# Chunk stage of a retention / RWKV-7 / mixture-of-experts layer: the kept state enters PSUM by a product with the identity, and VectorE scales the sum in one operation

## The reference, cut to what matters

```python
def step(s, xt):
    wt, kt, vt, kkt, at = xt[:5]
    sa = jnp.einsum('bhvk,bhk->bhv', s, -kkt)
    s = (s * wt[:, :, None, :] + sa[..., None] * (kkt * at)[:, :, None, :]
         + vt[..., None] * kt[:, :, None, :])
    return s, jnp.einsum('bhvk,bhk->bhv', s, xt[5])
```

## Time and profile before

| | |
|---|---|
| median of three runs | 4093.11 us |
| lowest, highest | 4092.32, 4101.29 us |
| span of the profiled execution, first to last instruction | 4080.9 us |
| TensorE (matmul) busy | 3706.6 us, 91% |
| VectorE busy | 2310.9 us, 57% |
| ScalarE busy | 1890.7 us, 46% |
| GpSimd busy | 663.1 us, 16% |
| chunk stage | about 1192 to 2192 us of the span |

### The profile page before, as it was taken

The page is one execution under the profiler, slowest core; times in us unless marked ns, Lnnn a source line. Parts: engine busy times, 40 slices in busy tenths (PEclk is TensorE's granted clock), DMA queues, the critical chain, the costliest instruction groups (busy, mean ns, idle before and its releaser), DMA issues. The chain is left out here.

```text
span 4080.9 us, 96351 instructions
## 1 busy us (share of the span) xinstructions
PE 3706.6 (91%) x40786; PEld 3108.5 (76%) x40786; DVE 2310.9 (57%) x3792; ACT 1890.7 (46%) x3029; POOL 663.1 (16%) x637
## 2 busy tenths in 40 slices
PE   7999999999978888888887979997699999999993
PEld 6778878888867777777786867785588888888883
DVE  6533523434348888888786964555544444454545
ACT  5533434433336665666565443333244444444443
POOL 1000000000012222222220333200011111111111
PEclk9999999999989999999999989998799999999996
DMA  7555554444442222322323366644366666666668
GB/s 279 192 181 192 180 192 157 150 160 158 150 129 77 80 70 74 81 81 76 92 65 115 103 228 225 198 169 184 137 214 216 213 218 207 214 207 214 213 211 298
DMA packets 378754, 673.61 MB, mean 165 GB/s; under 512 B 90428, under 2 KB 261540, under 8 KB 360712
## 3 DMA queue, kind: packets, MB, share of 16 engines
q1 hardware_dynamic: 351368, 580.69, 42.9%
q0 software_dynamic: 27008, 87.46, 7.3%
HBM read 524.89 MB, written 143.15 MB: 164 GB/s over the span
## 5 line engine op out<-in xcount | busy, mean ns | idle before, releaser
L112 PE MATMUL fro__acc<-fro__hT_hi,fro__wh 128*128 128x512 f32 (+1 forms) x1608 | 625.2, 389 | 11.8 <-DVE fro__hT_lo L2692 8.9
L113 PE MATMUL fro__acc<-fro__hT_hi,fro__wl 128*128 128x512 f32 (+1 forms) x1608 | 613.2, 381 | 0.0
L114 PE MATMUL fro__acc<-fro__hT_lo,fro__wh 128*128 128x512 f32 (+1 forms) x1608 | 613.1, 381 | 0.0
L2698 DVE TENSOR_TENSOR fro__wl<-prj__w,fro__wh 128x1024 fp32r<-128x1024 f32 x201 | 246.2, 1225 | 637.5 <-ACT fro__wh L2481 637.5
L2109 DVE TENSOR_TENSOR fin__wl<-fin__raw,fin__wh 128x4096 fp32r<-128x4096 f32 x96 | 424.7, 4424 | 316.3 <-ACT fin__wh L2053 316.3
L2053 ACT ACTIVATE fin__wh<-fin__raw 128x4096 fp32r<-128x4096 f32 x96 | 348.4, 3629 | 190.4 <-PE exp__acc L114 190.3
L112 PE MATMUL exp__acc<-fin__wh,exp__xh 128*128 128x512 f32 x1024 | 400.1, 391 | 0.7 <-DVE exp__xl L2114 0.7
L114 PE MATMUL exp__acc<-fin__wl,exp__xh 128*128 128x512 f32 x1024 | 398.7, 389 | 0.0
L113 PE MATMUL exp__acc<-fin__wh,exp__xl 128*128 128x512 f32 x1024 | 398.7, 389 | 0.0
L112 PEld LDWEIGHTS fro__acc<-fro__hT_hi,fro__wh 128*128 128x128 f32 x1608 | 303.7, 189 | 77.8 <-issue 22.2
L113 PEld LDWEIGHTS fro__acc<-fro__hT_hi,fro__wl 128*128 128x128 f32 x1608 | 303.8, 189 | 59.0 <-issue 3.6
(11 more groups left out here) (461 smaller groups left out, 7648.3 us busy)
## 6 DMA issues: line engine op xcount, KB each, us to landing
fin__raw<-in_w_x SPq DMA_DIRECT2D x96, 2048.0 KB
prj__w<-in_w_z SPq DMA_DIRECT2D x201, 512.0 KB, 3.9
s_zT<-fro__pool SPq DMA_DIRECT2D x128, 256.0 KB, 4.3
fro__wm<-in_w_mod POOLq DMA_DIRECT2D x16, 1024.0 KB, 5.5
mix__gate<-s_zT SPq DMA_DIRECT2D x64, 256.0 KB, 3.9
prj__xin<-in_tokens SPq DMA_DIRECT2D x18, 512.0 KB, 5.6
rwc__kS<-s_kS SPq DMA_DIRECT2D x36, 256.0 KB, 3.1
rwc__kkn<-s_kkn SPq DMA_DIRECT2D x36, 256.0 KB, 3.2
```

The costliest lines, as they stand in the source:

```text
L112: pe.matmul(out, sh, mh, start=first, stop=False)
L113: pe.matmul(out, sl, mh, start=False, stop=False)
L114: return pe.matmul(out, sh, ml, start=False, stop=last)
L2698: ve.tensor_tensor(wl[s % 3][:, :, :], w[s % 3][:, :, :], wh[s % 3][:, :, :], ALU.subtract).then_inc(split_lo, 1)
```

## The change

The scaled state no longer stays on VectorE's side of the addition. A new function `kept_state` on TensorE multiplies the identity by `Hb` (two products, one for each half of the partitions, 64 rows by 256 columns, float32) and opens the accumulation in `EB` with it; the 16 products of `state` then add onto it. VectorE's `state` becomes one multiplication, from `EB` and `F` into `Hb`. The tensors `H` and the signals `hadd0` and `hadd1` are gone; those who waited for `hadd` now wait for `hup`. The waits for `gd` and for the other block's signal move from `state` into `kept_state`.

`kept_state(h-2, 1)` is placed behind `refine(2, p, 1)` and in front of `double(1, h)`; `kept_state(p, 0)` behind `solve(p, 0)` and in front of `double(3, h)`.

```diff
-        H = [sb(f"H{d}", [P, 4, WD]) for d in range(2)]
...
                 ve.wait_ge(S[f"sm{t}"], at(f"sm{t}", j))
-                tt(H[d][:, :, :], EB[:, 0:256].rearrange("p (q c) -> p q c", q=4), Hb[d][:, :, :], ALU.add).then_inc(S[f"hadd{t}"], 1)
                 ve.wait_ge(S["fex"], at("fex", u))
-                ve.wait_ge(S[f"hadd{t}"], at(f"hadd{t}", j))
-                tt(Hb[d][:, :, :], H[d][:, :, :], F[u % B][:, k, :, :], ALU.mult).then_inc(S[f"hup{t}"], 1)
+                tt(Hb[d][:, :, :], EB[:, 0:256].rearrange("p (q c) -> p q c", q=4), F[u % B][:, k, :, :], ALU.mult).then_inc(S[f"hup{t}"], 1)
...
                 if g == 0 and j:
-                    pe.wait_ge(S["hadd0"], at("hadd0", j - 1))
+                    pe.wait_ge(S["hup0"], at("hup0", j - 1))
...
+            def kept_state(j, t):
+                pe.wait_ge(S["gd"], at("gd", j + t))
+                if t == 0 and exists(j - 1) and exists(j + 1):
+                    pe.wait_ge(S["hup1"], at("hup1", j - 1))
+                for r in map(side, range(2)):
+                    m = mm(EB[r, 0:256], ident[r, r], Hb[j % 2][r, :, :].rearrange("p q c -> p (q c)"), start=True, stop=False, skip_group_check=True)
+                m.then_inc(S[f"km{t}"], 1)
+
             def state(j, t):
                 u, s = j % B, turn_of(j, t)
                 pe.wait_ge(S[f"uc{t}"], at(f"uc{t}", j))
-                pe.wait_ge(S["gd"], at("gd", j + t))
-                if t == 0 and exists(j - 1) and exists(j + 1):
-                    pe.wait_ge(S["hadd1"], at("hadd1", j - 1))
+                if s:
+                    pe.wait_ge(S[f"km{t}"], at(f"km{t}", j))
                 for key, val in ((kappa_t[u], v_t[u]), (beta_t[u], U[t])):
...
-                                   start=(val is not U[t] and q == 0), stop=val is U[t], skip_group_check=True)
+                                   start=False, stop=val is U[t], skip_group_check=True)
...
                 if exists(p):
                     refine(2, p, 0)
                     refine(2, p, 1)
+                if exists(h - 2) and exists(h):
+                    kept_state(h - 2, 1)
                 if inverting:
                     double(1, h)
...
                 if exists(p):
                     solve(p, 0)
+                    kept_state(p, 0)
                 if inverting:
                     double(3, h)
```

More of the change, by code:

```diff
@@ L202, in rwkv_chunks @@
         lds, lws, low_in = [[sem(f"{n}{d}") for d in range(2)] for n in ("lds", "lws", "low_in")]
-        N = dict(um=1, am=1, m1=2, trm=3, bonm=1, t0m=2, xm=2 * LEV, tm=2 * LEV, ttm=LEV, em=2, gm=6, vm0=1, vm1=1, rhm0=1, rhm1=1, uum0=1, uum1=1, ym0=1, ym1=1, sm0=1, sm1=1,
-                 m1d=4, xb0=2, tt0=2, xd=2 * LEV, ed=2, erc=2, gd=6, hadd0=1, hadd1=1, hup0=1, hup1=1,
+        N = dict(um=1, am=1, m1=2, trm=3, bonm=1, t0m=2, xm=2 * LEV, tm=2 * LEV, ttm=LEV, em=2, gm=6, vm0=1, vm1=1, rhm0=1, rhm1=1, uum0=1, uum1=1, ym0=1, ym1=1, sm0=1, sm1=1, km0=1, km1=1,
+                 m1d=4, xb0=2, tt0=2, xd=2 * LEV, ed=2, erc=2, gd=6, hup0=1, hup1=1,
                  scan=1, kd1=1, dd=1, kd2=1, dd2=1, bd=1, fld=1, dld=1, betad=1, kappad=1,
```

## The result

Fifteen executions of each kernel on one chip gave a median of 4092.02 us before and 4106.33 us after: ratio **1.0032, 95% interval 1.0024 to 1.0041**, slower by some 14 us (the interval is 10 to 17), more than the 0.2% that a measurement here can tell. The forecast was 4115.5 us, +22.4.

The account below looks back on a forecast made before the run. No engine fills the chunk stage; waits between TensorE and VectorE bound each turn. Per turn +1.00 - 0.34 = +0.66 us, over 34 turns +22.4 on 4093.1, gives 4115.5 us; range 4098 to 4132.

Parts of the forecast that it names:

- -0.34 us: VectorE, one operation fewer per update: mask of level 4 comes 0.34 us earlier per turn, not the apparent 1.26.
- L581 takes 1.1 to 1.2: Sign of being right: VectorE's scaled_lower, behind the state update, takes 1.1 to 1.2 us in place of 1.75.
- L589's two halves take 1.4 to 1.8: Sign of being right: VectorE's two halves before the level 4 mask take 1.4 to 1.8 us, not 1.06.
- I take 0.49: TensorE: the two added float32 products into EB take 0.49 us together, between 0.43 and 0.98.
- no overlap: Rival, 8%: TensorE's two new products follow each other, taking 0.98 us; 16.7 us more in all, 4132.
- `couple(2, h)` comes later by 0.49 + 0.51 = 1.00: TensorE after the wait for Gr: new products (0.49) and double(1, h) (0.51) delay couple(2, h) by 1.00 us.
- `kept_state(p, 0)` costs nothing: TensorE, first block: the new products take the place of the idle 0.40 us in front of double(3, h).
- I put the second update at 0: VectorE, between the halves of masked: its removed operation gains 0, since ScalarE bounds what follows.
- The sum: +0.66 x 34 = 22.4: Whole chain: +1.00 - 0.34 = +0.66 us per turn, in 34 turns +22.4 us.
- the new multiplication is held: Rival, 4%: VectorE's multiplication of EB by F is held, nothing saved; +34 us, 4127.
- hidden wait: Rival, 15%: Gr is already there when TensorE reaches the new products, only their 0.49 added; 5.1 us, 4098.
- gaps filled: Rival, 9%: longer waits let TensorE's "issue" gaps, 36.3 us together, catch up; all gone gives -13.9 us, 4079.

Follow-up runs that it names:

- a1: Changed kernel without the identity products, TensorE's code as before, VectorE's one operation, kept state left out; 4084.25 us, 0.9975 of the kernel before.
- a3: Kernel before, still two VectorE operations per update, but the second reads EB (PSUM) instead of H, kept state left out; 4079.5 us, ratio 0.9962.
- c3: Kernel before, but VectorE adds Hb into EB in place, then multiplies EB by F into Hb, TensorE unchanged; 4083.6 us, ratio 0.9965.
- b4: Changed kernel without the products of kept_state(p, 0), waits unchanged, that kept state left out; 4104.32 us, 1.0034 of the kernel before.
- a2: Changed kernel with kept_state(h-2, 1) and its wait put behind double(1, h); 4097.89 us, 1.001 of the kernel before.
- a4: Changed kernel where kept_state(h-2, 1) keeps its wait in front of double(1, h) but issues no products; 4092.99 us, 0.9993 of the kernel before.
- c1: Changed kernel with the second update summed in the free half of XB[1] instead of EB; 4091.14 us, 1.0002 of the kernel before.
- b1: Kernel before with GpSimd's bonus(h+1) moved behind its other work of the turn; 4080.18 us, ratio 0.9974.
- c4: c3 with GpSimd's bonus moved behind its other work, as in b1; 4081.99 us, 0.9967 of the kernel before.

## Why the prediction came out as it did

The direction held, the two causes (the products and the moved wait, less a small gain on VectorE) are the ones that the runs show, and the time fell inside the range, 9 us below the point. The term for `couple(2, h)` was too large, and one of the terms of nothing was right for a wrong reason. Step by step:

- **"-0.34 us" for VectorE:** -0.33 in the profile. That the removed 1.24 us would mostly not arrive, because the hold passes to `scaled_lower` and L589, was right: 0.33 of the apparent 1.26 did. a1 prices it at 10 us, and 0.33 x 34 is 11.
- **"L581 takes 1.1 to 1.2":** wrong, and against the text's own times. It measured 1.69 (1663 ns mean). The forecast had it start at 2087.62 and end at 2089.22, which is 1.60. Its end was right; the 1.2 belongs to a kernel with an operation in front of it that uses up 0.5 us of the same hold, and a3 and c3 show just that: 1.16. Nothing in the sum hung on it.
- **"L589's two halves take 1.4 to 1.8":** 1.91 in the turn shown, and the beta half's mean went from 629 before to 1013 ns. Right in kind, slightly more held.
- **"I take 0.49" for the products:** 0.48 from the first new product to `double` (1498.31 to 1498.79), 0.43 the second time. The records take 0.378 each, and four of them are through in 0.48 us. One product alone takes at least 0.43 by the forecast's own rate, two in a row would take 0.86, so the two products overlap:

```profile
L867 PE MATMUL rwc__EB<-rwc__Hb,hold__ident x268: 375/378/687, 1254.5 to 2173.3; 64*64 64x256 f32 x134
```

- **The rival "no overlap" (8%), 0.98:** ruled out by that row and the 0.48 us. The Trainium skill's "Different row tiles cannot access same PSUM bank simultaneously" (TensorEngine Tiling (Array Packing), Gotcha 1: PSUM Pressure) did not delay them. The two products lie on the diagonal and write different halves of the partitions of `EB`. The Trainium skill's PSUM page (PSUM — Partial Sum Buffer, PSUM bank collisions raise a hardware error) counts a collision of two such writes by one bank within one quadrant of 32 partitions, which these two never share.
- **"`couple(2, h)` comes later by 0.49 + 0.51 = 1.00":** the term that was mis-sized; it measures 0.78 in the even turns and 0.90 in the odd ones, 0.84 in the mean. In an even turn there are now 1.69 us from the end of `Gr` to `couple(2, h)` (1498.25 to 1499.94); before 0.91, with `Gr` ending at 2084.50:

```profile
2084.09 0.41 DVE L627 TENSOR_TENSOR rwc__Gr<-rwc__PB,rwc__TTm 128x256 f32<-128x256 f32 x1
```

  That is +0.78. The products are the 0.48. `double(1, h)` adds 0.39, not 0.51: `state` starts at 1499.18, while the last group of `double` is still being issued, since its float32 products are let in among it (the rows with x2 and x6 above). And the first product starts 0.06 behind the end of `Gr`, where `state` started 0.15 behind it. 0.48 + 0.39 - 0.09 = 0.78. So "strictly in the order written" does not hold for the starts in the trace: records of one function can start among those of the function before it, and those of `couple(2, h)` did so at 2085.41 in the kernel before.

  In an odd turn nothing is let in. Before, then after:

```profile
2110.32 0.42 DVE L627 TENSOR_TENSOR rwc__Gr<-rwc__PB,rwc__TTm 128x256 f32<-128x256 f32 x1
2110.89 0.68 PE L875 MATMUL rwc__EB<-rwc__v_t,rwc__kappa_t 64*64 64x64 f32 x16
2111.84 0.41 PE L783 MATMUL rwc__XB<-rwc__Tb,rwc__ATb 64*64 64x64 bf16 x15
```

```profile
1524.44 0.41 DVE L626 TENSOR_TENSOR rwc__Gr<-rwc__PB,rwc__TTm 128x256 f32<-128x256 f32 x1
1524.91 0.65 PE L867 MATMUL rwc__EB<-rwc__Hb,hold__ident 64*64 64x256 f32 x4 [1.02 <-DVE rwc__Gr L626]
1525.39 0.29 PE L790 MATMUL rwc__TP<-rwc__Xb,rwc__TTb 64*64 64x64 bf16 x8
1525.90 0.66 PE L879 MATMUL rwc__EB<-rwc__v_t,rwc__kappa_t 64*64 64x64 f32 x16
1526.86 0.42 PE L780 MATMUL rwc__XB<-rwc__Tb,rwc__ATb 64*64 64x64 bf16 x16
```

  There `double(1, h)` adds the whole 0.51 (1525.39 to 1525.90), and the 1.10 us from the end of `Gr` to `couple(2, h)` become 2.00. In the even turns these products of `state` read one half of the partitions and write the other (`r = side(e ^ s)` with s = 1), in the odd turns they stay in their half, as `double` does. That this decides who is let in is a reading of the two kinds of turn, not a test.
- **"`kept_state(p, 0)` costs nothing":** b4 shows it, within its interval, but the reason given was wrong. It was to take the place of TensorE's idle time in front of `double(3, h)`, "larger after the change because the mask of level 3 comes earlier". An earlier mask leaves less idle time, not more: before there is a median of 0.65 us, in a1, which has the earlier mask and no products, more than 0.05 us in only 1 of 33 turns. The products fill no gap; they are hidden because VectorE is late for the mask of level 4. The text had named that cover too, with "about 0.2 us to spare"; TensorE waits there 0.64 us in the median. That the term still came out as 0 is luck in part.
- **"I put the second update at 0":** not tried alone, but the waits bear it out. VectorE is ready earlier and then waits 0.9 us for ScalarE's `ATb` in 33 turns, 30.3 us where it was 0.9, and `ATb` starts 0.49 us behind `sg` as before (1514.03 to 1514.52).
- **"The sum: +0.66 x 34 = 22.4":** with 0.84 for 1.00 and 0.33 for 0.34 it is +0.51 x 34 = 17 us, beside 14.3 timed. The moved wait was called "the larger part"; it isn't. Of the 0.84 the products are 0.48 and the move 0.36, and a2 and a4 give the products 14 to 16 us and the move 7 to 9.
- **The rival "the new multiplication is held" (4%):** ruled out; L633 took 411 to 419 ns in all its 66 records from 1250 to 2180 us.
- **The rival "hidden wait" (15%):** the 22 of 34 turns were indeed no sign of cover: after shows the wait in 33.
- **The rival "gaps filled" (9%):** the three profiles with the moved wait have the fewest issue gaps, 30.2 (after), 29.6 (a4) and 33.4 us (b4); the eleven others 36.3 to 53.2. So the gaps do shrink where TensorE waits longer, by 3 to 14 us against the two profiles of before, whose own difference is 7. But the sum above is only some 3 us larger than the timed loss, less than the interval of the ratio can tell, so little or none of it reached the end. That instructions come no faster than TensorE takes them was the reason given for them; no run here tests it.

## What to carry to other kernels

Before an operation is removed to save its time, ask why it takes that long: if it stands in a hold by another engine, its neighbour takes the hold over, and changing the kind of its operands (one input in PSUM, c3) can be worth as much as removing it and puts no product on another engine. Where new work opens an accumulation, its wait moves to the place of that work; put it behind everything that does not need the buffer (a2 against after, 9 us for one line's place). If the work gets a buffer of its own, count the waits that the new place brings (c1: 0.4 us in every second turn). And read a held operation by its end, not its length.

## What the runs showed of the hardware

- **VectorE and GpSimd.** An operation of VectorE with two inputs in SBUF beside GpSimd's tensor operations ends a fixed time after GpSimd's: 0.28 us for 128 x 256, 0.54 for 64 x 512; GpSimd's next (128 x 512) ends 1.12 to 1.15 behind VectorE's. With one input in PSUM it is not held (0.42 in every one of a3's and c3's records, and 0.41 to 0.42 for the new L633). The same 0.54 to 0.55 shows at `key2` (128 x 512) in b1 and c4. This fits an exclusive turn for each operation, and agrees with the Trainium skill (SBUF — State Buffer, SBUF: two separate sides): two SBUF inputs on VectorE against a GpSimd operation that reads SBUF, whichever starts first having the ports for the whole instruction.
- **An operation that reads and writes the same PSUM bank** on VectorE ran as fast as one that writes SBUF (0.424 against 0.416 us).
- **Two float32 products of 64 x 256 in one PSUM bank, on the diagonal of the array, overlap:** 0.48 us to the next instruction behind a wait, 0.43 without one.
- **Products can start among those written before them:** the first of `state` at 1499.18, the last six of `double` from 1499.20. Between these two functions it is seen in the even turns, not in the odd ones.
- **TensorE has gaps with no releaser,** 30 to 53 us in 930. The three kernels that keep it waiting longest have the fewest, but they do not decide the time: c3 has the most (53.2) and is among the fastest. This was not expected in that size, and its cause is open.
